# Stage b of an eight-stage block: passes written out, work placed beside a pass's last head, four banks for the gate products, gate through tanh

## What is computed

```python
proj = h @ w_in                       # h = rms_norm(x, gain)
qkv = proj[..., :9216]  # q, k, v  x  3 patterns  x  8 heads  x  128
z = proj[..., 9216:]    # 8 heads x 128
for g, (window, dilation) in enumerate(((128, 1), (512, 4), (2048, 16))):
    q = rotary(rms_norm(qkv[:, :, 0, g])); k = rotary(rms_norm(qkv[:, :, 1, g]))
    o, lse = dilated_window_attention(q, k, qkv[:, :, 2, g], window // dilation, dilation)
o = sum of the three o, weighted with softmax(lse)       # one softmax over all three
x = x + (o * silu(z)) @ w_out
```

## Time and profile before

| | |
|---|---|
| median of three runs | 3138.06 us (3137.13 to 3142.39) |
| profiled execution | 3136.17 us, its span 3134.3 us |
| PE busy | 2940.8 us (94% of the span) |
| DVE, ACT, POOL busy | 1774.4, 1107.3, 269.2 us |
| mean granted clock of PE | 0.965 |

### The profile page before, as it was taken

The page is one execution under the profiler, slowest core; times in us unless marked ns, Lnnn a source line. Parts: engine busy times, 40 slices in busy tenths (PEclk is TensorE's granted clock), DMA queues, the critical chain, the costliest instruction groups (busy, mean ns, idle before and its releaser), DMA issues.

```text
span 3134.3 us, 39236 instructions
## 1 busy us (share of the span) xinstructions
PE 2940.8 (94%) x14032; PEld 2416.0 (77%) x14032; DVE 1774.4 (57%) x2633; ACT 1107.3 (35%) x1620; POOL 269.2 (9%) x247
## 2 busy tenths in 40 slices
PE   8999999988999899999999988699999878899998
PEld 6888888877887678878888865488888744788887
DVE  5555536653576466654555586765344568464445
ACT  4332324443354432223422444443222423442222
POOL 1000000000000000000000061220000444010001
PEclk9999999999999899999999999699999988999999
DMA  4322322112211123223232321023222210122222
GB/s 141 108 91 84 108 88 68 61 54 68 75 55 61 54 97 99 95 94 97 85 101 87 104 69 44 14 75 108 96 98 94 88 34 14 41 89 99 96 99 87
DMA packets 70410, 252.22 MB, mean 80 GB/s; under 512 B 7808, under 2 KB 9856, under 8 KB 69632
## 3 DMA queue, kind: packets, MB, share of 16 engines
q1 hardware_dynamic: 68112, 241.89, 23.3%
q10 hardware_dynamic: 2160, 8.49, 0.8%
HBM read 248.25 MB, written 2.10 MB: 80 GB/s over the span
## 4 chain that ended last, share of the span: by engine, by line
PE 81%; DVE 8%; issue 4%; POOL 3%; ACT 2%; DMA 0%; DVEq 0%; ACTq 0%; POOLq 0%
PE ps L296 18%; PE ps L298 18%; PE ps L297 18%; PE ps L567 2%; PE ps L568 2%; PE ps L569 2%; PE ps L767 1%; POOL arena L1953 1%; PE ps L768 1%; PE ps L769 1%; PE ps L810 1%; PE ps L796 1%; DVE w_low L283 1%; PE ps L590 1%; PE ps L828 1%
## 5 line engine op out<-in xcount | busy, mean ns | idle before, releaser
L283 DVE TENSOR_TENSOR w_low<-raw,w_high 128x1024 fp32r<-128x1024 f32 x456 | 566.8, 1248 | 427.1 <-ACT w_high L276 417.8
L296 PE MATMUL ps<-h_high,w_high 128*128 128x512 f32 x1872 | 742.6, 397 | 26.3 <-DVE root L1001 10.2
L297 PE MATMUL ps<-h_low,w_high 128*128 128x512 f32 x1872 | 733.8, 392 | 0.0
L298 PE MATMUL ps<-h_high,w_low 128*128 128x512 f32 x1872 | 733.4, 392 | 0.0
L276 ACT ACTIVATE w_high<-raw 128x1024 fp32r<-128x1024 f32 x456 | 478.2, 1051 | 438.7 <-PE ps L298 214.3
L296 PEld LDWEIGHTS ps<-h_high,w_high 128*128 128x128 f32 x1872 | 354.9, 190 | 103.0 <-issue 28.5
L298 PEld LDWEIGHTS ps<-h_high,w_low 128*128 128x128 f32 x1872 | 354.6, 189 | 74.6
L297 PEld LDWEIGHTS ps<-h_low,w_high 128*128 128x128 f32 x1872 | 355.1, 190 | 70.9
L296 PE MATMUL ps<-y_high,w_high 128*128 128x512 f32 x688 | 270.4, 393 | 0.7 <-DVE y_low L1797 0.4
L297 PE MATMUL ps<-y_low,w_high 128*128 128x512 f32 x688 | 268.6, 390 | 0.0
L298 PE MATMUL ps<-y_high,w_low 128*128 128x512 f32 x688 | 268.4, 390 | 0.0
(11 more groups left out here) (391 smaller groups left out, 4577.8 us busy)
## 6 DMA issues: line engine op xcount, KB each, us to landing
raw<-stream SPq DMA_DIRECT2D x456, 512.0 KB, 3.4
table<-tables_in ACTq DMA_DIRECT2D x5, 1088.0 KB, 5.9
x<-x_in ACTq DMA_DIRECT2D x8, 256.0 KB, 8.4
x_out<-x SPq DMA_DIRECT2D x16, 128.0 KB, 1.7
const<-const_in SPq DMA_DIRECT2D x1, 673.0 KB, 8.3
work<-ssm_in ACTq DMA_DIRECT2D x1, 512.0 KB, 3.6
params<-params_in ACTq DMA_DIRECT2D x1, 287.0 KB, 6.8
```

The lines of the kernel that those rows point to most:

```text
L283: nc.vector.tensor_tensor(w_low[:, u.slot], raw[:, u.raw], w_high[:, u.slot].bitcast(F32), ALU.subtract).then_inc(weights_low, 1)
L296: nc.tensor.matmul(bank, wh, high[:, k], start=k == 0, stop=False)
L297: nc.tensor.matmul(bank, wh, low[:, k], start=False, stop=False)
L298: mm = nc.tensor.matmul(bank, wl, high[:, k], start=False, stop=k == tiles - 1)
```

## The change

Both passes are written out in Python, `for i in range(2)`. Gate m goes to bank m; DVE takes it at the start of slot (4, m+1), ahead of that slot's softmax. The gate is formed as z (tanh(z/2) + 1) times half of the attention output, one DVE instruction more for each gate. The three slots without a unit get one of 24 matmuls each: in pass 0 the first three value units of pass 1 (banks 0 to 3), in pass 1 k = 0 to 5 of output tiles 0 to 3 together (banks 0 to 3); k = 6 and 7 of these follow behind, then tiles 4 to 7 one by one in banks 6, 7, 6, 7. The splits move with them, and the wait for y_low before pass 1 stands one pattern later. The core of the diff:

```diff
+        B_TAIL = [(BH, 4), (BH, 5), (BH + 1, 0)]
+        B_BANKS = (0, 1, 2, 3, 6, 7, 6, 7)
+        def b_split_unit(first, i, j, u):
+            if b_unit(first, i, j, u) is not None:
+                return b_unit(first, i, j, u)
+            n = B_TAIL.index((j, u))
+            return Unit(first + B_HALF * (i + 1) + n) if i == 0 or n == 0 else None
...
+            def values(i, g, kk):
+                    if g == 1 and i == 1 and k == 0:
+                        pe.wait_ge(y_low_done, y_base + BH)
+                    for b in range(NBLK):
+                        if k == 0 and g == 0 and i == 1:
+                            pe.wait_ge(b_z_taken, b + 1)
...
+            def out_tile(m, k):
+                u = Unit(first + 2 * B_HALF + m)
+                if k == 0:
+                    pe.wait_ge(weights_low, u.count(1))
+                    pe.wait_ge(b_z_taken, BH + m + 1)
+                if m == 0:
+                    pe.wait_ge(y_low_done, y_base + k + 1)
...
-            with pe.Fori(0, 2) as i:
-                pe.wait_ge(y_low_done, lin(y_base, i, BH))
+            for i in range(2):
...
+                        elif u == 2:
+                            pe.wait_ge(b_args, lin(2 * BH, i, 2 * BH))
                         else:
-                            pe.wait_ge(b_z_taken, lin(u - 1, i, BH))
-                        product(pe, unit, ps[:, n % 2], h_high, h_low)
+                            pe.wait_ge(b_k_done, lin(3 * BH, i, 3 * BH))
+                        product(pe, unit, ps[:, u if j == BH else n % 2], h_high, h_low)
+                    elif i == 0:
+                        values(1, 0, B_TAIL.index((j, u)))
+                    else:
+                        for k in (2 * B_TAIL.index((j, u)), 2 * B_TAIL.index((j, u)) + 1):
+                            for m in range(4):
+                                out_tile(m, k)
...
-            out_product(pe, o, first + 2 * B_HALF, y_base, r=r, last=last, following=following)
+            for m in range(4):
+                out_tile(m, KD - 2)
+            for m in range(4):
+                out_tile(m, KD - 1).then_inc(units_done, 1)
+            for m in range(4, KD):
+                if m >= 6:
+                    pe.wait_ge(out_free, 8 * o + m + 1)
+                product(pe, Unit(first + 2 * B_HALF + m), ps[:, B_BANKS[m]], y_high, y_low)
...
-                        nc.scalar.activation(b_szs[m % 2][:], b_szs[m % 2][:], ACT.Silu).then_inc(b_silu, 1)
+                        nc.scalar.activation(b_tanh, b_szs[m % 2][:], ACT.Tanh, scale=0.5).then_inc(b_silu, 1)
...
-                    nc.vector.tensor_tensor(full[:, j % 2], source, b_szs[j % 2][:], ALU.mult).then_inc(b_gated, 1)
+                    nc.vector.scalar_tensor_tensor(out=b_szs[m % 2][:], in0=b_tanh, scalar=1.0, in1=b_szs[m % 2][:],
+                                                   op0=ALU.add, op1=ALU.mult).then_inc(b_gated, 1)
+                    nc.vector.scalar_tensor_tensor(out=full[:, m % 2], in0=b_szs[m % 2][:], scalar=0.5, in1=source,
+                                                   op0=ALU.mult, op1=ALU.mult).then_inc(b_gated, 1)
```

More of the change, by code:

```diff
@@ new lines, in b_tensor @@
+        def b_tensor(pe, t, first, o, y_base, r, last=False, following=None):
+            def values(i, g, kk):
+                u = Unit(first + 4 * g + kk, i, B_HALF)
+                pe.wait_ge(weights_low, u.count(1))
+                for kl in range(2):
+                    k = 2 * kk + kl
+                    wh = w_high[:, u.slot, kl * T:(kl + 1) * T]
+                    wl = w_low[:, u.slot, kl * T:(kl + 1) * T]
+                    if g == 0 and i == 0:
+                        pe.wait_ge(h_low_done, t + k + 1)
+                    if g == 1 and i == 1 and k == 0:
[3 more added lines that the diff above has]
+                            pe.wait_ge(b_z_taken, b + 1)
+                        if k == 0 and g == 2:
+                            pe.wait_ge(b_v_copied, 12 * i + b + 1)
+                        bank = ps[:, 4 * (g % 2) + b]
+                        hh, hl = b_blk(h_high[:, k], b), b_blk(h_low[:, k], b)
+                        nc.tensor.matmul(bank, hh, wh, start=k == 0, stop=False)
+                        nc.tensor.matmul(bank, hh, wl, start=False, stop=False)
+                        mm = nc.tensor.matmul(bank, hl, wh, start=False, stop=k == KD - 1)
+                mm.then_inc(units_done, 1)
+            def out_tile(m, k):
+                u = Unit(first + 2 * B_HALF + m)
+                if k == 0:
+                    pe.wait_ge(weights_low, u.count(1))
+                    pe.wait_ge(b_z_taken, BH + m + 1)
+                if m == 0:
+                    pe.wait_ge(y_low_done, y_base + k + 1)
+                wh, wl = w_high[:, u.slot, k * P:(k + 1) * P], w_low[:, u.slot, k * P:(k + 1) * P]
+                bank = ps[:, B_BANKS[m]]
+                nc.tensor.matmul(bank, wh, y_high[:, k], start=k == 0, stop=False)
+                nc.tensor.matmul(bank, wh, y_low[:, k], start=False, stop=False)
+                return nc.tensor.matmul(bank, wl, y_high[:, k], start=False, stop=k == KD - 1)
@@ L771, in b_tensor @@
+                        if i == 0 or 4 * g + kk >= len(B_TAIL):
+                            values(i, g, kk)
                 for j, u in B_SLOTS:
```

93 lines of the change are left out of this document (52 added, 41 removed).

## The result

| | before | changed |
|---|---|---|
| median | 3139.91 us (4 runs, 3137.13 to 3142.39) | 3116.94 us (4 runs, 3116.35 to 3117.44) |
| profiled execution, its span | 3136.17, 3134.3 us | 3117.01, 3115.2 us |

The ratio is 0.9927 [0.991, 0.9944]: the changed kernel is 0.7% faster, and its median lies 1.6 us under the forecast of 3118.5. The two profiled spans differ by 19.1 us.

The account below looks back on a forecast made before the run. PE was busy 94% of the span, so only its standstills, in stage b's tails, could pay. Gains of 18.1 and 1.1 sum to 19.2 us, 3136.17 to 3117.0; median with skipped spread 3118.5, range 3107 to 3127.

Parts of the forecast that it names:

- Pass 0: First pass's tail: two 5.12 us PE waits go, one of 8 us comes in slot (4, 4); gain 18.1 us.
- slot on DVE: Length of a tail slot: softmax 4.35, two gate instructions 1.4, from `full` 2.98, take 0.6; together 9.3 us.
- rival 2: Tail gates: each gate instruction 1.085 and ACT 0.8 more, 13 us lost in all, time 3132; chance 0.08.
- Pass 1: Second tail and output stage: waits of 8, 2.9 and 5.2 us, loop 5.2 us a tile; gain 1.1 us.
- skipped spread: Spread of norms skipped in pass 1: worth under 1 us, left out of the sum of gains.
- of the 18 won by 51.2, the output stage gives back 17: Pass 1, 51.2 us behind its first tail softmax: 18 us won, of which the queue of takes loses 17.
- zero: Start of the softmax in slot (4, 1), from which the forecast counts a pass's times; 676.82 in pass 0.
- No new wait: Slot (4, 4): DVE has gate 3 at 19.9, each pass saves another 8 + 2.3 us, time 3098; chance 0.06.
- Longer gate chain: Tail gates: chain 1.6 us longer in three slots and at the end, gain 6, time 3132; chance 0.08.
- The clock: Tails and output stage: PE stays at 1.2 GHz after the first idle stretch, 61 us more, 3180; chance 0.04.
- Nothing gained: Output stage: its loop takes 7.5 us a tile in place of 5.2, gain 5, time 3133; chance 0.05.
- the change undone by table loads: Loads ahead of Tanh in the tails start gates 1.1 us later: three slots, two passes, 7 us, time 3125.

Follow-up runs that it names:

- e_values: The changed kernel with pass 1's output tiles put back as before and only the moved value units of pass 0 kept; 3105.43 us, ratio 0.989.
- e_unroll: The kernel before with stage b's two passes written out on PE, ACT and DVE, nothing else changed; 3138.34 us, ratio 0.9994.
- e_early: The changed kernel with DVE taking gate 3 right behind gate 2, one slot earlier, in slot (4, 3); 3107.22 us, ratio 0.9899.
- e_late3: e_early with pass 1's output tile 3 joining one slot later, in slot (4, 5); 3099.8 us, ratio 0.9872.
- e_silu: The changed kernel with Silu in place of Tanh, the two DVE gate instructions kept in number and size; 3125.96 us, ratio 0.9958.
- e_banks: The changed kernel without units in the three slots; values and output tiles stand where they stood before; 3109.04 us, ratio 0.9903.
- e_loop: The changed kernel, but in the output loop ACT splits unit m+4 before squaring tile m and DVE takes tile m before its split; 3112.02 us, ratio 0.9917.
- e_best: e_late3 and e_loop together; 3092.7 us, ratio 0.9853 to the kernel before.
- e_loop_again: e_loop run once more, unchanged; 3111.15 us, ratio 0.9911 to the kernel before.

## Why the prediction was right

**Pass 0: right in each step.** Measured times stand first, the forecast ones in brackets. Counted from the first tail softmax, the gate product 3 ends and slot (4, 4) begins at 17.2 (forecast 17.8), the wait ends at 27.3 (27.95) after 7.85 (8), PV ends at 50.9 (51.2); gain 18.3 (18.1). The term mis-sized is the slot on DVE, 9.07 in place of 9.3: the rows had priced the step from `full` to the take at 2.98, and it takes 2.79, and the softmax 4.27 in place of 4.35. Of these 0.27, 0.08 each are instructions that start before the listed end of the one ahead, and 0.09 is `y_high`, which starts 0.04 behind `full` where it was 0.13. The value taken for the gate instructions, 0.69 and not the 1.085 of the earlier trace rows, was measured at 0.68 (L973). The profile of the kernel before had a nearer row than the one that served as the bound, the same operation sixteen times at 0.69 (view by line), and with it rival 2 had less for it than it seemed:

```profile
L1345 DVE SCALAR_TENSOR_TENSOR arena<-arena 128x512 f32<-128x512 f32 x16 | 11.1, 692 | 0.5
```

**Pass 1: right in mechanism, each wait a little shorter.** k = 7 starts at 54.1 (54.4), product 4 at 59.7 (60.0) after 2.60 (2.9), product 6 at 76.8 (77.3) after 4.28 (5.2), take 7 ends at 92.1 (92.9). The loop is 5.15 us a tile (5.2) and the clock costs 1.7 behind product 4's wait (1.3). Gain 1.9 (1.1 and up to 1 for the skipped spread). One sentence was wrong beside the sum: "of the 18 won by 51.2, the output stage gives back 17" took pass 0's gain for pass 1. Without pass 0's wait for y_low it is some 14 won and 12 given back. The sum did not use it, since it went by the end of take 7. That the output tiles as placed gain nothing, e_values shows by another way: without them pass 1 is 10.6 us shorter.

**The sum was right partly by chance.** Two terms that it did not have cancel nearly. The changed kernel comes to the first tail 2.14 us later than before: 1.27 of it is already there at stage b's first softmax, in a stretch that the change does not touch, where the kernels here lie between 0.6 us sooner and 1.9 later than the one before; 0.87 comes up to the tail (e_unroll has the same 0.9 there, so it comes from writing the passes out, which the prediction counted at nothing). Behind take 7, stage c's norm starts 1.3 sooner than before (5.87 against 7.13 from the take's start). Then 20.2 gained from zero to take 7, less 2.14, plus 1.3, less 0.2 in the later stages, is the measured 19.1; the forecast had 19.2. It is luck too that the median lies so near: the forecast put 1.9 us between profile and median, from three runs of the kernel before, and for the changed kernel the two are equal to 0.1.

**The rivals.** *No new wait* falls as a forecast; but its price is confirmed, and corrected in one point. It counted 10.3 us for each pass from an earlier take. e_early measured 9.7 for the two together, all of it in pass 0, since in pass 1 the split of output unit 3 holds the same slot; with both locks off (e_late3) it is 17: 9.8 in pass 0 and 8.5 in pass 1 by the table. *Longer gate chain* falls with L973. *The clock* falls: PE was back at full speed within the same product after each wait, 12 matmuls behind 7.85 us and some nine behind 2.60, and the granted clock of the output stage was 0.93. *Nothing gained* falls with the loop of 5.15. Of *the change undone by table loads*, forecast at 7 us, e_silu measured 7.1 in the two passes and 9 in the median.

**Where the gain comes from** was not told apart by the prediction, and the runs do so: written-out passes nothing; four banks with the early take and the later wait for y_low 20 us, of which an estimate gives 4 to the last; tanh 8 to 9; value units in pass 0 one to three (pass 0, and the medians of e_values and e_banks); output tiles in pass 1 minus 11. The prediction named the new wait and the loop that these 11 are made of, but not that the change would be better without this part.

**Open:** the 2 to 3 us that e_loop loses in later stages (seen twice, and not in e_best), the 2 that e_silu costs beyond the two passes, and how the 20 us divide among banks, early take and y_low's wait.

## What to carry to other kernels

Work put into a stall must be free of every lock of that moment: here the unit chosen needed the one bank that was released last, so the stall moved into the new work, and in one pass a second lock (the slot of a weight unit) stood behind the first, to be seen only when that was gone. List for the moved instruction each semaphore it waits for, with the time at which it is signalled, not only the last. And finishing four tiles at once instead of one after another hands the stall on to whoever takes them: follow the moved work to its last consumer before counting the gain.

## What was not expected of the hardware

In e_loop a round of the output loop takes 3.78 to 3.85 us, of which DVE's h_low has 1.5, twice its usual length. Timeline of DVE and POOL in e_loop:

```profile
1052.16 0.75 DVE L449 SCALAR_TENSOR_TENSOR h_low<-x,params,h_high 128x512 fp32r<-128x512 f32 x1
...
1053.82 1.21 DVE L283 TENSOR_TENSOR w_low<-raw,w_high 128x1024 fp32r<-128x1024 f32 x1
...
1054.66 1.53 POOL L324 TENSOR_TENSOR root<-root,ssq 128x512 f32<-128x512 f32 x1 [671.20 <-ACT ssq L312]
...
1055.23 1.52 DVE L449 SCALAR_TENSOR_TENSOR h_low<-x,params,h_high 128x512 fp32r<-128x512 f32 x1 [0.19 <-ACT h_high L443]
```

and of POOL in the changed kernel, where it runs while DVE has nothing to do:

```profile
1058.46 1.28 POOL L324 TENSOR_TENSOR root<-root,ssq 128x512 f32<-128x512 f32 x1 [673.50 <-ACT ssq L312]
```

POOL's instruction lasts 1.53 us in place of 1.28, and ends 1.16 behind the end of the split (1055.03) that DVE had under way; h_low, started meanwhile, lasts 1.52 in place of 0.75 and ends 0.56 behind POOL's end (1056.19). That reads as one standing still for the other, not as both going slower; it is argued from the ends, not shown. The Trainium skill, "SBUF — State Buffer", section Who interferes with whom, states such a lock between a DVE instruction with two SBUF inputs and a GpSimd instruction that reads SBUF; both DVE instructions here have two. Six of the eight h_low of e_loop's output stage last 1.51 or 1.52 us, where the eight of the changed kernel have a mean of 0.746. The six are those that begin while a POOL instruction runs; the other two, at 1052.16 and 1079.05, last 0.75. e_loop_again shows the same six, one of them 1.72 beside a POOL instruction of 1.74, and the same two. No run here took POOL's instruction away to test it.
